# Down projection of a two-layer decoder trunk by seven block products over pairs of inner tiles

## The chip, the cores and the metric

The kernel runs on one core of one Trainium2 chip. Its time is the device time of one execution in microseconds (us); the median of three executions is given. TensorE does the matmuls (PE in the profile), with its weight loads beside them (PEld). VectorE is DVE, ScalarE is ACT, GpSimd is POOL, and SyncE (SP) issues most of the transfers.

## What is computed

The trunk has two layers over 1024 positions and 1024 channels. Each layer is a mixer followed by a gated MLP with a causal width-3 convolution. The change touches the MLP, above all its last product:

```python
def conv_ffn(x, norm_g, w_up, conv_w, conv_b, w_down):
    h = causal_depthwise_conv(rms_norm(x, norm_g) @ w_up, conv_w, conv_b)
    g, u = jnp.split(h, 2, axis=-1)
    return (jax.nn.silu(g) * u) @ w_down          # D_FF = 2816: 22 inner tiles of 128
...
for layer in range(2):
    x = x + mixer(layer, x)
    x = x + conv_ffn(x, ...)
```

## The kernel before

Activations lie transposed, channels on the partitions and positions along the row. All large products are float32 in two parts: a value is cut into a high part (rounded to the PE's fp32r) and a low part (the rest), and a product is three matmuls, high by high, high by low, low by high. A matmul is 128x128 weights by 512 positions.

**Weights.** SP loads 128x1024 tiles into a ring of three (`w_raw`), each after the tile three before it has been used up (L2029, L2056). ACT makes the high part (`w_hi`), POOL the low part (`w_lo`), both into rings of three tiles, which the MLP uses as six half tiles.

**Up projection** (`pe_ffn`, 22 steps j in each layer). A step makes gate rows and value rows of one inner tile. It is a 2x2 block product done with seven block products in place of eight: a11, s2, s3, s1, a22, a12, s4, in this order (`PRODS`). Each is 12 matmuls (`pe_product`, L1695). Their weights are quarters of two weight tiles (g and u) or sums s1 to s4 of quarters, which POOL makes (L1639 to L1664). ACT cuts the high parts (`act_cut`, L1631), POOL the low ones (`pool_low`, L1637). A half tile is cut when the product six before it is done, so the cuts run up to six products ahead.

**Behind the products** DVE adds the seven results into rows: ACT copies a11 to `ffn_v` (`act_p1`, L1845); DVE makes the U sums `dve_u2` and `dve_u3` (L1776, L1781), then the gate rows (`c22`, `c21`, `hg`: L1789, L1794, L1800) and the value rows (`c11`, `c12`, `hu`: L1809, L1813, L1820). Then comes the convolution: the centre tap on ACT (`act_center`, L1854) and two more taps on DVE (`dve_taps`, L1826 and L1828) for the gate side (m = 0) and the value side (m = 1); SiLU on ACT (L1860); the gating on DVE (`dve_gated`, L1835). Each engine's order is written out in `dve_ffn` and `act_ffn`. Two waits of PE matter below: product a22 of step j needs `dve_u3` of step j, and s1 of step j+1 needs `c12` of step j:

```python
            elif name == "a22":
                pe.wait_ge(parts, l * ALL_PARTS + part(j, "u3"))
```

ACT's order around it is, for step j: a cut, SiLU of j-1, `act_p1` of j (which waits for `c12` of j-1), the cut of s4 of j, the centre tap of the value side of j-1, the cut of a11 of j+1.

**Gated rows.** There are two buffers `ffn_gated` on the chip, so SP writes 20 of the 22 gated tiles to DRAM (`sp_gated_out`, L2061), between its two weight loads of a step, and they are read back for the down projection (`gated_in`).

**Down projection** (`pe_down`, L1748). The 22 inner tiles are taken in chunks of 4, 4, 4, 4, 2, 4. For each chunk and each of 8 output tiles PE adds up the chunk in PSUM, in one of four rooms in turn, and DVE adds the room to the residual `res` (`dve_down`, L1911, 48 per layer in the whole). Each inner tile is cut into high (ACT, L1876) and low (DVE, L1839); weights by ACT (L1891) and POOL (L1896). Layer 1 begins as output tiles of layer 0's last chunk are final: ACT and DVE normalise them, POOL adds squares (L438) and cuts the first weight tile of the mixer (L2039, L2041).

Of the kernel before, what the change touches and what calls it, by code (L numbers as in the profile page):

```python
# [14 lines left out]
P = 128  # L15
# [14 lines left out]
DOWN_ORDER = (FC - 2, 0, 1, 2, FC - 1, *range(3, FC - 2))  # L30
DOWN_SIZES = (4, 4, 4, 4, 2, 4)
LAST = len(DOWN_SIZES) - 1
ML_DV = 256
# [43 lines left out]
def program(nc, x_in, pos_in, wall, pool_w, params, lam4, consts, scratch, gated_rows, out):  # L77
    with ExitStack() as ctx:
# [188 lines left out]
        def td(n):  # L267

            return n - sum(min(max(n - t, 0), 2 * FC) for t in (T_FFN0, T_FFN1))
# [1120 lines left out]
        def act_pair_base(act, f, p):  # L1390

            if p:
                act.wait_ge(tt_made, f.l * 3 * KC // 2 + 3 * p - 1)
            evacuated(act, jobs[f"out{f.l}", 2 * p])
            act.activation(rbc[:, :], res[:, 2 * p, :], ACT.Copy, scale=gain(f, 2 * p)).then_inc(t_base, 1)

        def act_pair_high(act, f, p):

            act.wait_ge(tt_made, f.l * 3 * KC // 2 + 3 * p + 3)
# [53 lines left out]
        def dve_pair_sums(dve, f, p):  # L1453
# [52 lines left out]
        SLOTS = 8  # L1506
        STAGED = [p for p in range(FC) if DOWN_ORDER[p] < FC - 2]
# [17 lines left out]
        ALL_PARTS = len(FIRST_PARTS) + len(PARTS) * (FC - 1)  # L1525

# [3 lines left out]
        class Ffn:  # L1530


            def __init__(self, l):
# [20 lines left out]
                self.a = [at(f"ffn_gated{l}_{i}", [P, S], F32, r) for i, r in enumerate((r_m1, r_m2))]  # L1554
                self.hi = at(f"act_hi_buf{l}", [P, SLOTS, S], F32R, far)
                self.lo = at(f"act_lo_buf{l}", [P, SLOTS, S], F32R, far + 8 * K4)
                self.stage = at(f"act_stage{l}", [P, 2 * STAGES, S], F32, near)
                self.A = pj[:, self.late, 0:HALF]
# [12 lines left out]
            def g_tile(self, j):  # L1571

                return self.T0 + 2 * j + (j == 0)

            def u_tile(self, j):

                return self.T0 + 2 * j + (j != 0)

            def cut(self, t, w):

                q = (2 * (self.T0 % W_RING) + t) % (2 * W_RING)
# [28 lines left out]
            def gated_source(self, p):  # L1610

                if p in STAGED:
                    return self.stage[:, 2 * (STAGED.index(p) % STAGES), :]
                return self.a[DOWN_ORDER[p] % 2][:, :]
# [4 lines left out]
        def act_cut(act, f, t):  # L1619

            j, i = divmod(t, N_PROD)
            name = (PRODS if j else FIRST_PRODS)[i]
            if t < 2 * W_RING:
                act.wait_ge(tile_done, td(f.T0 - W_RING + t // 2 + 1))
            else:
                act.wait_ge(prod_done, f.l * N_PROD * FC + t - 2 * W_RING + 1)
            if name[0] == "a":
                raw_landed(act, f.g_tile(j) if name == "a22" else f.u_tile(j))
            else:
                act.wait_ge(s_made, f.l * 4 * FC + 4 * j + int(name[1]))  # L1630
# [16 lines left out]
        def pool_s2(pool, f, j):  # L1647
            raw_landed(pool, f.u_tile(j))
            pool.wait_ge(s_made, f.l * 4 * FC + 4 * j + 1)
            if j:  # L1650
                pool.wait_ge(c_ready, f.l * N_PROD * FC + prod(j - 1, "s2"))
            pool.tensor_tensor(wsum[1][:, :], wsum[0][:, :], f.source(j, "a11"), ALU.subtract).then_inc(s_made, 1)  # L1652

        def pool_s3(pool, f, j):
            raw_landed(pool, f.g_tile(j))
            raw_landed(pool, f.u_tile(j))
            if j:
                pool.wait_ge(c_ready, f.l * N_PROD * FC + prod(j - 1, "s3"))
            pool.tensor_tensor(wsum[2][:, :], f.source(j, "a11"), f.source(j, "a21"), ALU.subtract).then_inc(s_made, 1)  # L1659

        def pool_s4(pool, f, j):
            pool.wait_ge(s_made, f.l * 4 * FC + 4 * j + 3)
            pool.wait_ge(c_ready, f.l * N_PROD * FC + prod(j, "s1"))
            pool.tensor_tensor(wsum[0][:, :], f.source(j, "a12"), wsum[1][:, :], ALU.subtract).then_inc(s_made, 1)  # L1664

        def pe_room(pe, f, j, name):

            l = f.l
            if name == "a12":
                pe.wait_ge(p1_copied, l * FC + j + 1)  # L1670
            elif j and name == "s4":
                pe.wait_ge(parts, l * ALL_PARTS + part(j, "c22"))
# [1437 lines left out]
```

## Time and profile before

| | us |
|---|---|
| median of 3 executions (2168.45 to 2169.01) | 2168.55 |
| the profiled execution's own time | 2168.64 |
| its span in the trace | 2166.8 |
| PE busy | 2148.5 |
| DVE busy | 1326.5 |
| POOL busy | 1073.1 |
| ACT busy | 838.9 |

The span is that of the instructions; the time has 1.8 us around it. Matmuls are pipelined: the duration of one (389 ns) overlaps the next, so the rate is read from start to start. The granted TensorE clock is 0.997 of full speed over the whole span.

### The profile page before, as it was taken

What the parts mean: (1) busy time and instruction counts of PE and PEld (TensorE: products, weight loads), DVE (VectorE), ACT (ScalarE), POOL (GpSimd) and SP (SyncE); (2) the same over time, 40 slices, a digit from 0 to 9 for tenths busy, and PEclk for the clock granted to TensorE, in tenths of its full rate; (3) what the DMA queues carried; (4) which work ended last, traced back from release to release, by engine and by line L of the source; (5) the groups of instructions that cost most, each with busy time, mean ns of one, the idle gap of its engine ahead of it and who ended that gap; (6) DMA issues with size and microseconds to landing.
All of it is one profiled execution on the core that took longest, in us unless ns stands there. A gap on an engine that the chain in (4) does not pass through costs nothing. (4 is left out here: it accounts for less than half of the span.)

```text
span 2166.8 us, 26682 instructions
## 1 busy us (share of the span) xinstructions
PE 2148.5 (99%) x10219; PEld 1773.2 (82%) x10219; DVE 1326.5 (61%) x1425; ACT 838.9 (39%) x1312; POOL 1073.1 (50%) x664
## 2 busy tenths in 40 slices
PE   9999999999999999999999999999999999999999
PEld 8777778878888888888888898887788888888887
DVE  7766777567777777444544244286777777774442
ACT  6555452444443443111344433434444444441110
POOL 2222117677777773222543333267777777742220
PEclk9999999999999999999999999999999999999999
DMA  6111104022222224222321021030222222242221
GB/s 205 59 50 33 42 10 143 23 87 88 78 80 80 84 88 155 98 89 73 111 84 59 20 79 59 20 137 29 78 86 80 78 88 88 69 156 97 97 68 78
DMA packets 50429, 174.80 MB, mean 81 GB/s; under 512 B 6080, under 2 KB 8192, under 8 KB 50304
## 3 DMA queue, kind: packets, MB, share of 16 engines
q1 hardware_dynamic: 42816, 147.49, 20.5%
q10 hardware_dynamic: 7488, 25.61, 3.2%
q8 instruction: 82, 1.34, 0.3%
q14 instruction: 43, 0.35, 0.1%
HBM read 139.23 MB, written 29.66 MB: 78 GB/s over the span
## 5 line engine op out<-in xcount | busy, mean ns | idle before, releaser
L2039 POOL TENSOR_TENSOR w_hi<-w_raw,ones 128x1024 fp32r<-128x1024 f32 x54 | 106.1, 1965 | 494.1 <-PE pj L328 170.5
L1637 POOL TENSOR_TENSOR w_lo<-w_sum,w_hi 128x512 fp32r<-128x512 f32 x176 | 270.2, 1545 | 106.4 <-ACT w_hi L1631 106.4
L1896 POOL TENSOR_TENSOR w_lo<-w_raw,w_hi 128x1024 fp32r<-128x1024 f32 x44 | 106.0, 2409 | 342.0 <-ACT w_hi L1891 342.0
L1631 ACT ACTIVATE w_hi<-w_sum 128x512 fp32r<-128x512 f32 x176 | 106.6, 628 | 299.5 <-POOL w_sum L1652 170.3
L1706 PE MATMUL pj<-t_hi,w_hi 128*128 128x512 f32 x520 | 205.4, 395 | 7.6 <-DVE ffn_v L1781 7.6
L1706 PE MATMUL pj<-t_lo,w_hi 128*128 128x512 f32 x520 | 204.7, 394 | 0.0
L1706 PE MATMUL pj<-t_hi,w_lo 128*128 128x512 f32 x520 | 204.3, 393 | 0.0
L1637 POOL TENSOR_TENSOR w_lo<-w_raw,w_hi 128x512 fp32r<-128x512 f32 x132 | 172.7, 1309 | 63.4 <-ACT w_hi L1631 63.4
L1891 ACT ACTIVATE w_hi<-w_raw 128x1024 fp32r<-128x1024 f32 x44 | 46.6, 1059 | 318.7 <-PE dn L1748 168.7
L1706 PE MATMUL pj<-xa_hi,w_hi 128*128 128x512 f32 x348 | 135.8, 390 | 1.5 <-DVE xa_lo L1450 0.9
L1706 PE MATMUL pj<-xb_hi,w_hi 128*128 128x512 f32 x348 | 135.6, 390 | 1.6 <-DVE xb_lo L1450 0.9
L2041 POOL TENSOR_TENSOR w_lo<-w_raw,w_hi 128x1024 fp32r<-128x1024 f32 x54 | 135.0, 2501 | 4.2
L1706 PE MATMUL pj<-xa_hi,w_lo 128*128 128x512 f32 x348 | 135.4, 389 | 0.0
L1706 PE MATMUL pj<-xb_hi,w_lo 128*128 128x512 f32 x348 | 135.4, 389 | 0.0
L1706 PE MATMUL pj<-xa_lo,w_hi 128*128 128x512 f32 x348 | 135.4, 389 | 0.0
L1706 PE MATMUL pj<-xb_lo,w_hi 128*128 128x512 f32 x348 | 135.4, 389 | 0.0
L1839 DVE TENSOR_TENSOR act_lo_buf<-act_stage,act_hi_buf 128x1024 fp32r<-128x1024 f32 x40 | 80.2, 2009 | 80.0 <-ACT act_hi_buf L1876 80.0
L355 PE MATMUL pj<-xb_hi,w_hi 128*128 128x512 f32 x384 | 128.2, 415 | 0.0
L1631 ACT ACTIVATE w_hi<-w_raw 128x512 fp32r<-128x512 f32 x132 | 83.2, 631 | 113.6 <-PE pj L1706 113.6
L1706 PEld LDWEIGHTS pj<-t_hi,w_hi 128*128 128x128 f32 x520 | 98.7, 190 | 33.6 <-issue 9.1
L355 PE MATMUL pj<-xb_lo,w_hi 128*128 128x512 f32 x384 | 119.2, 392 | 0.0
L355 PE MATMUL pj<-xb_hi,w_lo 128*128 128x512 f32 x384 | 118.4, 390 | 0.0
(390 smaller groups left out, 5519.2 us busy)
## 6 DMA issues: line engine op xcount, KB each, us to landing
w_raw<-weights SPq DMA_DIRECT2D x187, 512.0 KB, 3.5
gated_rows<-ffn_gated SPq DMA_DIRECT2D x40, 512.0 KB, 2.6
act_stage<-gated_rows ACTq DMA_DIRECT2D x32, 512.0 KB, 4.5
x_first<-x_t SPq DMA_DIRECT2D x8, 512.0 KB, 7.7
res<-x_t SPq DMA_DIRECT2D x8, 512.0 KB, 6.6
act_stage<-gated_rows SPq DMA_DIRECT2D x8, 512.0 KB, 5.5
scratch<-res ACTq DMA_DIRECT2D x8, 512.0 KB, 2.6
res<-scratch SPq DMA_DIRECT2D x8, 512.0 KB, 7.0
```

The source lines that it names most:

```text
L355: ins = pe.matmul(o[:, t * HALF:(t + 1) * HALF], w, x[:, k, t * HALF:(t + 1) * HALF], start=(first and m == 0), stop=(last and m == 2))
L1631: act.activation(f.cut(t, whi), f.source(j, name), ACT.Copy).then_inc(c_high, 1)
L1637: pool.tensor_tensor(f.cut(t, wlo), f.source(j, name), f.cut(t, whi).bitcast(F32), ALU.subtract).then_inc(c_ready, 1)
L1706: ins = pe.matmul(o, f.cut(t, w)[:, k * P:(k + 1) * P], f.moving(name, x, k), start=(not more and k == 0 and q == 0), stop=(k == KC // 2 - ...
L1839: dve.tensor_tensor(f.lo[:, p % SLOTS, :], f.gated_source(p), f.hi[:, p % SLOTS, :].bitcast(F32), ALU.subtract).then_inc(act_lo, 1)
L1891: act.activation(whi[:, n % W_RING, :], raw[:, n % RAW_RING, :], ACT.Copy).then_inc(w_high, 1)
L1896: pool.tensor_tensor(wlo[:, n % W_RING, :], raw[:, n % RAW_RING, :], whi[:, n % W_RING, :].bitcast(F32), ALU.subtract).then_inc(w_ready, 1)
L2039: pool.tensor_tensor(whi[:, w, :], raw[:, r, :], ones[:, 0:1].to_broadcast([P, D]), ALU.mult).then_inc(w_high, 1)
L2041: pool.tensor_tensor(wlo[:, w, :], raw[:, r, :], whi[:, w, :].bitcast(F32), ALU.subtract).then_inc(w_ready, 1)
```

## The change

Inner tiles 4 to 19 (16 of 22) leave the plain chunks and are taken as 8 pairs. The plain chunks that stay are one of 4 inner tiles (20, 0, 1, 2) at the start and one of 2 (3 and 21) at the end. Two pairs and half of the output rows make a block: 8 blocks m per layer, each seven block products of 12 matmuls in the order `PRODS` (`pe_block`). Their weights are cut and summed by the same functions as the up projection's, whose steps j now run from 0 to 29.

- **Pair sums (T sums).** The moving side also needs sums. In the even steps j = 6 to 20 DVE makes four 128x512 sums in place in the two gated buffers (`dve_pair_t`), between the gate side's taps and `c12`. SP writes the two buffers out again (`sp_pair_out`, two transfers), between the step's two weight loads, the first after three sums, the second after four.
- **U sums first.** `dve_u2` and `dve_u3` of step j stand ahead of the gating of j-1. SP's write of a gated tile stands ahead of both weight loads of a step, no longer between them.
- **In the blocks** DVE adds each product into `u` or `res` (`dve_block`, seven additions of 1024 a block; in the first two blocks ACT copies the first); in the last two blocks three more, `res` plus `u`. ACT reads the pairs back from DRAM (`act_pair_load`) and cuts 1536 and 2048 positions of a pair per block (`act_pair_split`); DVE makes their low parts (`dve_pair_low_half`) between the additions.

```diff
-DOWN_ORDER = (FC - 2, 0, 1, 2, FC - 1, *range(3, FC - 2))
-DOWN_SIZES = (4, 4, 4, 4, 2, 4)
+DOWN_ORDER = (FC - 2, 0, 1, 2, 3, FC - 1)
+DOWN_SIZES = (4, 2)
+PAIR0 = 4
+N_PAIR = 8
+N_BLOCK = N_PAIR
...
+        def pe_block(pe, f, m, name):
...
+            if name == "a12":
+                if m < 2:
+                    pe.wait_ge(p1_copied, l * (FC + 2) + FC + m + 1)
+                else:
+                    pe.wait_ge(parts, l * LAYER_PARTS + block_part(m, "u1"))
+            elif name == "a22":
+                pe.wait_ge(parts, l * LAYER_PARTS + block_part(m, "e22"))
+            elif name == "s4":
+                pe.wait_ge(parts, l * LAYER_PARTS + block_part(m, "c22"))
...
+            else:
+                pe.wait_ge(parts, l * LAYER_PARTS + block_part(m - 1, {"a11": "a11", "s2": "u2", "s3": "e21", "s1": "c12"}[name]))
...
+        def dve_pair_t(dve, f, r):
+
+            b11, b12, b21, b22 = (f.ab[:, i, h * HALF:(h + 1) * HALF] for i in range(2) for h in range(2))
...
+            dve.tensor_tensor(b22, b22, b12, ALU.subtract).then_inc(tt_made, 1)
+            dve.wait_ge(tt_made, at0 + 1)
+            dve.tensor_tensor(b12, b12, b11, ALU.subtract).then_inc(tt_made, 1)
+            dve.wait_ge(tt_made, at0 + 2)
+            dve.tensor_tensor(b11, b11, b22, ALU.add).then_inc(tt_made, 1)
+            dve.wait_ge(tt_made, at0 + 3)
+            dve.tensor_tensor(b21, b21, b11, ALU.subtract).then_inc(tt_made, 1)
...
+        def dve_block(dve, f, m):
+
+            u = f.u[m % 2][:, :, :]
+            if m >= 2:
...
+                dve_block_add(dve, f, m, "u1", u, f.block_room("a11"))
...
+            dve_block_add(dve, f, m, "u2", u, f.block_room("s2"))
+            if m >= N_BLOCK - 2:
+                dve_block_done(dve, f, m, "u2")
+                for row, half in ((1, 1), (1, 0), (0, 1)):
+                    to = f.res_of(m, row, half)
+                    dve.tensor_tensor(to, u, to, ALU.add).then_inc(parts, 1)
...
+            dve_block_add(dve, f, m, "e22", f.res_of(m, 1, 1), f.block_room("s3"))
...
+            dve_block_add(dve, f, m, "c22", f.res_of(m, 1, 1), f.block_room("s1"))
+            if m + 2 < N_PAIR:
+                dve_pair_low_half(dve, f, m + 2, 0)
...
+            dve_block_add(dve, f, m, "e21", f.res_of(m, 1, 0), f.block_room("a22"))
...
+            dve_block_add(dve, f, m, "a11", f.res_of(m, 0, 0), f.block_room("a12"))
+            if m + 2 < N_PAIR:
+                dve_pair_low_half(dve, f, m + 2, 1)
...
+            dve_block_add(dve, f, m, "c12", f.res_of(m, 0, 1), f.block_room("s4"))
...
                 if j > 1:
                     dve_u2(dve, f, j)
                     dve_u3(dve, f, j)
+                    dve_gated(dve, f, j - 1)
...
                 dve_taps(dve, f, j, 0)
+                if j >= PAIR0 + 2 and j % 2 == 0:
+                    dve_pair_t(dve, f, (j - PAIR0 - 2) // 2)
                 dve_c12(dve, f, j)
                 dve_hu(dve, f, j)
                 dve_taps(dve, f, j, 1)
-                dve_gated(dve, f, j)
...
             for j in range(FC):
-                sp_up_load(sp, f, f.T0 + 2 * j)
                 if j >= 3:
                     sp_gated_out(sp, f, j - 3)
-                sp_up_load(sp, f, f.T0 + 2 * j + 1)
+                sp_load(sp, f.T0 + 2 * j)
+                if j - 3 > PAIR0 and j % 2 == 0:
+                    sp_pair_out(sp, f, (j - 3 - PAIR0) // 2)
+                sp_load(sp, f.T0 + 2 * j + 1)
...
         def pool_cut(pool, n, s, per):
-            if n >= W_RING:
+            if n == T_MIX1:
+                pool.wait_ge(prod_done, N_PROD * N_UP)
+            elif n >= W_RING:
                 pool.wait_ge(tile_done, td(n - W_RING + 1))
```

DVE at the end of an even step and the start of the next, before (layer 0; the names stand in the section on the kernel before):

```order
L1828 SCALAR_TENSOR_TENSOR dn<-ffn_hg_129,params,dn 128x1023
L1813 TENSOR_TENSOR ffn_hu_132<-pj,ffn_v_0_130 128x512
L1820 TENSOR_TENSOR ffn_hu_132<-ffn_hu_132,rms_bc 128x512
L1826 SCALAR_TENSOR_TENSOR dn<-ffn_hu_132,params,dn 128x1022
L1828 SCALAR_TENSOR_TENSOR dn<-ffn_hu_132,params,dn 128x1023
L1835 TENSOR_TENSOR ffn_gated_0_134<-ffn_silu_133,dn 128x1024
L1776 TENSOR_TENSOR ffn_v_0_130<-pj,ffn_v_0_130 128x512
L1781 TENSOR_TENSOR ffn_v_1_131<-pj,ffn_v_0_130 128x512
```

and the same place of DVE in the change (L1935 to L1941 are the T sums, L1868 and L1873 the U sums):

```order
L1920 SCALAR_TENSOR_TENSOR dn<-ffn_hg_129,params,dn 128x1023
L1935 TENSOR_TENSOR ffn_gated_134<-ffn_gated_134 128x512
L1937 TENSOR_TENSOR ffn_gated_134<-ffn_gated_134 128x512
L1939 TENSOR_TENSOR ffn_gated_134<-ffn_gated_134 128x512
L1941 TENSOR_TENSOR ffn_gated_134<-ffn_gated_134 128x512
L1905 TENSOR_TENSOR ffn_hu_132<-pj,ffn_v_0_130 128x512
L1912 TENSOR_TENSOR ffn_hu_132<-ffn_hu_132,rms_bc 128x512
L1918 SCALAR_TENSOR_TENSOR dn<-ffn_hu_132,params,dn 128x1022
L1920 SCALAR_TENSOR_TENSOR dn<-ffn_hu_132,params,dn 128x1023
L1868 TENSOR_TENSOR ffn_v_0_130<-pj,ffn_v_0_130 128x512
L1873 TENSOR_TENSOR ffn_v_1_131<-pj,ffn_v_0_130 128x512
L1928 TENSOR_TENSOR ffn_gated_134<-ffn_silu_133,dn 128x1024
```

Four instructions were added ahead of `c12`, and the gating moved from ahead of the U sums to behind them.

ACT in one block of the change (L1689 cuts weights, L2082 cuts a pair, L2061 to L2064 read pairs back):

```order
L1689 ACTIVATE w_hi<-w_sum_118 128x512
L2061 DMA pair_stage_0_142<-gated_rows 128x2048
L1689 ACTIVATE w_hi<-w_raw 128x512
L2082 ACTIVATE pair_0_148<-pair_stage_0_142 128x1536
L1689 ACTIVATE w_hi<-w_sum_119 128x512
L1689 ACTIVATE w_hi<-w_sum_120 128x512
L2082 ACTIVATE pair_0_148<-pair_stage_0_142 128x2048
L1689 ACTIVATE w_hi<-w_sum_118 128x512
L2063 DMA pair_stage_0_142<-gated_rows 128x512
L2064 DMA pair_stage_0_142<-gated_rows 128x1024
```

The rows are the cuts of s4, a11, s2, s3 and s1; the pair's larger cut stands between those of s3 and s1, where the up projection has nothing.

## Rows read from the trace of the kernel before

**Rows 1.** The page, part 1: busy us of PE, share of the span, instructions
```profile
PE 2148.5 (99%) x10219; PEld 1773.2 (82%) x10219; DVE 1326.5 (61%) x1425; ACT 838.9 (39%) x1312; POOL 1073.1 (50%) x664
```
**Rows 2.** PE's waits: us in total, times, longest
```profile
PE pj L1706 <- DVE ffn_v L1781: 7.6, 4, 3.6
```
**Rows 3.** The chain that ended last, layer 1: start, us, what
```profile
1550.85 373.38 PE pj L1706 x1632
...
1935.14 10.88 PE dn L1748 x48
```
**Rows 4.** Timeline of PE, layer 1: start, duration, engine, line, what
```profile
1714.33 0.39 PE L1706 MATMUL pj<-xa_hi,w_hi 128*128 128x512 f32 x1
...
1725.22 0.39 PE L1706 MATMUL pj<-t_hi,w_hi 128*128 128x512 f32 x1
...
1733.40 0.39 PE L1706 MATMUL pj<-xa_hi,w_hi 128*128 128x512 f32 x1
```
**Rows 5.** Timeline of DVE in the same step
```profile
1714.90 1.29 DVE L1828 SCALAR_TENSOR_TENSOR dn<-ffn_hg,params,dn 128x1023 f32<-128x1023 f32 x1
1716.10 0.69 DVE L1813 TENSOR_TENSOR ffn_hu<-pj,ffn_v 128x512 f32<-128x512 f32 x1
1716.82 1.53 DVE L1820 TENSOR_TENSOR ffn_hu<-ffn_hu,rms_bc 128x512 f32<-128x512 f32 x1
...
1722.35 1.22 DVE L1835 TENSOR_TENSOR ffn_gated<-ffn_silu,dn 128x1024 f32<-128x1024 f32 x1
...
1724.28 0.69 DVE L1781 TENSOR_TENSOR ffn_v<-pj,ffn_v 128x512 f32<-128x512 f32 x1
```
**Rows 6.** Timeline of POOL in the same step
```profile
1715.24 1.30 POOL L1637 TENSOR_TENSOR w_lo<-w_raw,w_hi 128x512 fp32r<-128x512 f32 x1 [0.73 <-ACT w_hi L1631]
1716.50 1.30 POOL L1664 TENSOR_TENSOR w_sum<-w_raw,w_sum 128x512 f32<-128x512 f32 x1
```
**Rows 7.** Timeline of ACT in the same step
```profile
1717.25 0.60 ACT L1845 ACTIVATE ffn_v<-pj 128x512 f32<-128x512 f32 x1
1717.89 0.63 ACT L1631 ACTIVATE w_hi<-w_sum 128x512 fp32r<-128x512 f32 x1
1718.42 1.19 ACT L1854 ACTIVATE dn<-ffn_hu,params 128x1024 f32<-128x1024 f32 x1
```
**Rows 8.** PE in step 1 of layer 0, where it waited for a U sum
```profile
439.51 0.47 PE L1706 MATMUL pj<-t_hi,w_hi 128*128 128x512 f32 x1 [0.24 <-DVE ffn_v L1781]
```
**Rows 9.** Timeline of SP in the same step: issue of two weight loads
```profile
1714.54 3.66 SPq L2056 DMA_DIRECT2D w_raw<-weights  x2
```
**Rows 10.** The page, part 6: transfers, KB each, median us from issue to landing
```profile
w_raw<-weights SPq DMA_DIRECT2D x187, 512.0 KB, 3.5
gated_rows<-ffn_gated SPq DMA_DIRECT2D x40, 512.0 KB, 2.6
```
**Rows 11.** Timeline of POOL, steps 1 and 2 of layer 0: low part of s4
```profile
438.37 1.28 POOL L1637 TENSOR_TENSOR w_lo<-w_sum,w_hi 128x512 fp32r<-128x512 f32 x1 [0.81 <-ACT w_hi L1631]
...
455.83 1.30 POOL L1637 TENSOR_TENSOR w_lo<-w_sum,w_hi 128x512 fp32r<-128x512 f32 x1 [0.80 <-ACT w_hi L1631]
```
**Rows 12.** Groups of DVE by line and form: count, busy us, mean ns, idle before
```profile
L1911 DVE TENSOR_TENSOR res<-pj,res 128x1024 f32<-128x1024 f32 x48 | 57.9, 1219 | 92.9 <-PE pj L1748 92.9
...
L968 DVE TENSOR_TENSOR o_normed<-o_tok,o_rstd 128x1024 f32<-128x1024 f32 x4 | 4.9, 1225 | 0.1
```
**Rows 13.** Groups of ACT by line and form: the cut of a weight tile
```profile
L1891 ACT ACTIVATE w_hi<-w_raw 128x1024 fp32r<-128x1024 f32 x44 | 46.6, 1059 | 318.7 <-PE dn L1748 168.7 <-PE pj L1748 143.8 <-PE pj L1706 6.1
```
**Rows 14.** Timeline of POOL into layer 1: square sum, then the first weight cut
```profile
1062.08 2.61 POOL L438 TENSOR_TENSOR ssum<-ssum,sq_tmp 128x1024 f32<-128x1024 f32 x1 [2.83 <-ACT sq_tmp L426]
1064.66 1.89 POOL L2039 TENSOR_TENSOR w_hi<-w_raw,ones 128x1024 fp32r<-128x1024 f32 x1
1066.62 2.39 POOL L2041 TENSOR_TENSOR w_lo<-w_raw,w_hi 128x1024 fp32r<-128x1024 f32 x1
```
**Rows 15.** Timeline of PE: its first matmul of layer 1
```profile
1074.76 0.28 PE L2310 MATMUL pj<-w_hi,xb_hi 128*128 128x264 f32 x1
```

More of the change, by code:

```diff
@@ L1525, in program, with block_parts, block_part, act_at @@
         ALL_PARTS = len(FIRST_PARTS) + len(PARTS) * (FC - 1)
+        def block_parts(m):
+            shared = ("v22", "v21", "v12") if m >= N_BLOCK - 2 else ()
+            return ("u1",) * (m >= 2) + ("u2",) + shared + ("e22", "c22", "e21", "a11", "c12")
+        def block_part(m, name):
+            return ALL_PARTS + sum(len(block_parts(i)) for i in range(m)) + block_parts(m).index(name) + 1
+        LAYER_PARTS = block_part(N_BLOCK - 1, "c12")
+        def act_at(p):
+            return p if p < DOWN_SIZES[0] else p + 2 * N_PAIR
+        def pair_at(q, part):
+            return DOWN_SIZES[0] + 2 * q + part
+        def out_at(j):
+            return j + 1 + 2 * max(0, (j - PAIR0) // 2)
         def chunk_at(c):
@@ L1737, in pe_down @@
                     pe.wait_ge(gated, f.l * FC + FC)
+                elif c == LAST and d < 4:
+                    pe.wait_ge(parts, f.l * LAYER_PARTS + block_part(N_BLOCK - 1, ("a11", "u2", "e21", "c12")[d]))
                 else:
@@ L1791, in dve_c21 @@
         def dve_c21(dve, f, j):
[L1792 removed]
+            dve.wait_ge(prod_done, f.l * N_PROD * N_UP + prod(j, "a22"))
             if j:
@@ L3011, in ffn, with plain @@
         tiles = [up[FC], up[0]] + [up[FC * m + j] for j in range(1, FC) for m in range(2)]
-        at = 0
-        for size in DOWN_SIZES:
-            part = np.stack([down[i] for i in DOWN_ORDER[at:at + size]])
-            part = part.reshape(size, P, size, KC // size, P).transpose(2, 1, 3, 0, 4).reshape(size, P, D)
-            tiles += list(part)
-            at += size
+        def plain(order):
+            size = len(order)
+            part = np.stack([down[i] for i in order])
+            return list(part.reshape(size, P, size, KC // size, P).transpose(2, 1, 3, 0, 4).reshape(size, P, D))
+        tiles += plain(DOWN_ORDER[:DOWN_SIZES[0]])
+        blocks = down[PAIR0:PAIR0 + 2 * N_PAIR].reshape(N_PAIR // 2, 2, 2, P, 2, 2, 2, P)
+        for c in range(N_PAIR // 2):
+            for k in range(2):
+                for row in (1, 0):
+                    tiles.append(blocks[c][:, :, :, k, :, row].transpose(2, 1, 3, 0, 4).reshape(P, D))
+        tiles += plain(DOWN_ORDER[DOWN_SIZES[0]:])
         return tiles
```

382 lines of the change are left out of this document (268 added, 114 removed).

## The prediction

> **What bounds the kernel now.** I read the page first. PE is busy for 2148.5 of 2166.8 us with 10219 matmuls [rows 1], and the chain of waits is PE alone through the MLP of layer 1, up projection and down projection alike [rows 3]. So time goes only where PE gets fewer or cheaper matmuls, and every wait put on PE costs its full length. The rate is the same in both stages: 48 matmuls in 10.88 us are 0.2267 us each [rows 3], and one step of the up projection, 84 matmuls from 1714.33 to 1733.40, is 19.07 us or 0.2270 each [rows 4]; a product of 12 is 2.72 us.
>
> The view to read next is PE's waits. The one large entry is on `dve_u3`, 7.6 us in four waits [rows 2]; in step 1 PE started product a22 0.15 us after that sum's end [rows 8]. In the steady step the sum (L1781) ends at 1724.97 and a22 starts at 1725.22 [rows 4, 5]: PE does not wait, but only 0.25 us are left. The change works just ahead of this sum.
>
> **Removed from PE.** Per layer 16 inner tiles x 8 outputs x 6 = 768 matmuls become 8 blocks x 84 = 672. That is 192 fewer in the kernel, at 0.2267 us: **-43.5 us**. The rate has no reason to differ: each product is again 12 matmuls of 512, each with its own weight load, as in the up projection.
>
> **T sums (16 times).** I follow one step with the clock of the steady step, in which a22 starts at 1725.22. The last gate tap ends at 1716.19 [rows 5]. A T sum reads both inputs from SBUF, as `hu` (L1820) does. That row shows what it costs beside POOL: 1.53 us, ending 0.55 after POOL's operation of 1716.50 to 1717.80 [rows 5, 6]; an addition with one input in PSUM takes 0.69 [rows 5]. So DVE and POOL take turns. The first T sum waits for POOL's operation that ends at 1716.54 [rows 6] and ends at 1717.09; POOL's own sum then runs to 1718.35; the second T sum ends at 1718.9. After that POOL has nothing: its next operation needs ACT's cut [rows 11], which stands behind `act_p1`, which waits for `c12`, which is behind the T sums. The last two take 0.69 and 0.1 between them, to 1720.5. Then in order: `c12` 0.69 to 1721.1, ACT's copy 0.60 and cut 0.63 to 1722.4, centre tap 1.19 to 1723.55 [rows 7] (`hu` is done by then), two taps of 1.29 to 1726.2, two U sums to 1727.6 [rows 5], PE at 1727.75. Against 1725.22 that is 2.5 us. It counts the U sums ahead of the gating: with the 1.22 us of L1835 [rows 5] ahead of them it would be 3.7. So 16 x 2.5 = **+40 us**. Bounds: if no T sum meets POOL they take 3.1 in place of 4.3, and `hu` is hidden, 1.3 us a time, 21 in all; if all four meet a POOL operation, 7.2, that is 5.4 a time, 86 in all.
>
> The Trainium skill, page "SBUF — State Buffer", section "Who interferes with whom", says that a DVE instruction with two SBUF inputs and a GpSimd instruction reading SBUF hold the shared pair for the whole instruction, whoever was first. By that rule the turns cannot be shortened, and the upper bound is a rival below.
>
> **The load behind them (14 times).** SP issues the T sums' two writes between the two weight loads. The second load, issued at the step's start in the trace (1714.54) [rows 9], now comes after the fourth T sum, at about 1721.2, behind two writes (2.6 each alone) and 3.5 to land [rows 10]. I put landing at 1725.5 to 1726. ACT cuts it into a11 some 6 us late, and stands there, with its later centre tap of the gate side behind four more cuts that need POOL. By the same counting that tap is 2.1 us late; the next step's U sums, now ahead of the gating, have 1.3 us to spare. 0.8 us remain: **+11 us** (0 to 28, for 2 us each). The loads that now stand behind a gated write are 7 us later and are not needed for over 12: nothing.
>
> **The blocks (16).** POOL, per block: 11 operations of 1.26 [rows 6] and three waits for ACT's cut of a fresh sum, 0.8 each [rows 11]. From one low part of s4 to the next it did this in 17.46 us when not held by PE, with one DVE operation in between [rows 11]; PE needs 19.04. A block adds pair low parts of 1536 and 2048 positions: at the 1.225 of an undisturbed 1024 [rows 12] about 1.7 and 2.2 us in which POOL is shut out, where the up projection had 1.1 that showed; and ACT's cut of 2048, 1.9 us by the 1.06 for 1024 [rows 13], between its cuts of s3 and s1. Together a cycle comes to about 20.2, 1.1 more than PE's. The six half tiles of lead hold that for some five blocks (a12 is ready 11.4 us ahead); in the sixth PE waits 1.4. In the seventh DVE is about 4.5 us behind when it reaches the three extra additions, which have two SBUF inputs and take turns with POOL, 7 us in place of 3.7; a22 waits for `e22` behind them, 8 us by my count, and 3 more follow up to the block's end and in the eighth. That is 12 per layer, **+24 us**. Bounds: the three additions undisturbed still make `e22` 1 us late in each of two blocks, 4 in all; with reading back a pair (1.75 MB) delaying weight loads as well, 25 per layer, 50.
>
> **Into layer 1.** Output tiles of the last chunk become final every 2.72 us, no longer 5.44. POOL cuts layer 1's first weight tile after the square sum of the fourth tile: square 2.61, then 1.96 and 2.39, in the trace 5.8 us before PE's first matmul [rows 14, 15]. DVE needs 1.22 [rows 12] and about 1.5 per tile, as much as PE. I get POOL ready 4 us after PE: **+4 us** (0 to 6). The tail after the last matmul stays.
>
> Hidden: the first block's pairs are cut during the plain chunk of 43.5 us, where DVE had a third free; stores fit between tiles at 2.6 us each.
>
> **Sum.** -43.5 + 40 + 11 + 24 + 4 = +35.5. Against the profiled execution's own 2168.64 (the median is 2168.55, the same) that is **2204 us**.
>
> **Rivals.**
>
> *The other side: the T sums nearly hidden.* If POOL's phase leaves them alone (3.1 us, 21 in all), the late load is absorbed, and the blocks cost their least, the sum is -43.5 + 21 + 0 + 4 + 2 = -16.5: 2152; with the first two smaller still (0.75 a time is the least, if the taps start earlier) 2143. For it: 1.3 us of slack comes with the new order, and DVE is busy only 61% [rows 1]. Against it: `hu` meets POOL in every steady step. The deciding point is the wait per T sum: with the blocks and layer 1 as forecast and no late load, 1.0 us; with these at their least, 2.3. Chance 0.22.
>
> *T sums as forecast, the rest at its least.* -43.5 + 40 + 4 + 2 = +2.5: 2171. It needs a POOL cycle under 19. Chance 0.14.
>
> *All four T sums take turns*, by the lock whatever POOL's phase: -43.5 + 86 + 11 + 30 + 4 = +88: 2256. Against it: POOL runs dry behind `c12`. It is the case that the rule of the Trainium skill (page "SBUF — State Buffer", above) would give if POOL always had work. Chance 0.09.
>
> *The change does less than it says*: the order shows 1344 block matmuls for the 1536 taken out, so this could only be a rate above 0.2267. At 0.230 it would add 4 us. Too small for a case of its own.
>
> **How the numbers follow.** The forecast has 0.55, its own range 2180 to 2235. The whole range 2148 to 2240 leaves out most of the turns rival and the lowest part of the first. A difference of 0.2% (4.3 us) is about what can be told from none. Faster by more: 0.22, from the first rival and little of the second. Within: 0.08, from the second. Slower: 0.70.
>
> **What would show it.** PE's waits on `dve_u3` (now L1873), about 16 of 2.5 us in odd steps 7 to 21; with rows of 0.1 us or none, the T sum step is wrong. Smaller waits on it in even steps 8 to 20: the late load. T sums of about 0.8, 1.8, 0.7, 0.7 us. PE waits in the blocks from the sixth on, above all on `e22` of the seventh; none there, and the POOL cycle is wrong. A gap before layer 1's first matmul that POOL's L2041 ends. What would make the whole wrong is PE idle of under 40 us.

## The result and the profile after

The changed kernel takes 2207.47 us (median of four executions, 2205.56 to 2209.51), the kernel before on the same chip 2168.77. The ratio is 1.0181, with a 95% interval of 1.0167 to 1.0195. The forecast was 2204 us.

The page's busy times, which answer to [rows 1]:

```profile
PE 2128.8 (96%) x10027; PEld 1747.9 (79%) x10027; DVE 1428.8 (65%) x1545; ACT 890.0 (40%) x1396; POOL 1257.0 (57%) x808
```

PE has the 192 matmuls fewer, but is busy only 96% of the span. Its waits, which answer to [rows 2] (us in all, times, longest):

```profile
PE pj L1764 <- DVE ffn_v L1873: 46.6, 30, 2.3
PE dn L1839 <- DVE res L1954: 8.4, 4, 4.0
PE pj L1839 <- DVE pair L1950: 7.7, 4, 3.1
PE pj L2565 <- issue: 4.2, 1, 4.2
PE pj L1839 <- issue: 1.6, 1, 1.6
```

The first was 7.6 us in four waits. From PE's first matmul of a stage to the first of the next (for the last stage to the end of the span), the time went here:

| stage (us) | before | after |
|---|---|---|
| up projection, layer 0 / layer 1 | 431.0 / 431.2 | 459.1 / 457.3 |
| down projection, layer 0 / layer 1 | 239.4 / 242.7 | 233.7 / 233.0 |
| of it the eight blocks | none | 164.1 / 164.4 |
| mixer of layer 1 | 418.1 | 420.4 |

At their rate of 0.2267 us the 672 matmuls of the blocks would take 152.3 us. One step with T sums (j = 16) on DVE, in order of time (start, duration, line, operation, tiles, and in brackets the idle time ahead and what ended it):

```profile
758.54 0.99 DVE L1935 TENSOR_TENSOR ffn_gated<-ffn_gated 128x512 f32<-128x512 f32 x1
759.57 1.67 DVE L1937 TENSOR_TENSOR ffn_gated<-ffn_gated 128x512 f32<-128x512 f32 x1
761.27 0.69 DVE L1939 TENSOR_TENSOR ffn_gated<-ffn_gated 128x512 f32<-128x512 f32 x1
762.00 0.69 DVE L1941 TENSOR_TENSOR ffn_gated<-ffn_gated 128x512 f32<-128x512 f32 x1
762.61 0.68 DVE L1905 TENSOR_TENSOR ffn_hu<-pj,ffn_v 128x512 f32<-128x512 f32 x1
763.33 0.69 DVE L1912 TENSOR_TENSOR ffn_hu<-ffn_hu,rms_bc 128x512 f32<-128x512 f32 x1
765.64 1.29 DVE L1918 SCALAR_TENSOR_TENSOR dn<-ffn_hu,params,dn 128x1022 f32<-128x1022 f32 x1 [1.62 <-ACT dn L2022]
...
768.95 0.69 DVE L1873 TENSOR_TENSOR ffn_v<-pj,ffn_v 128x512 f32<-128x512 f32 x1
```

On PE, ACT and POOL of the same step:

```profile
769.78 0.47 PE L1764 MATMUL pj<-t_hi,w_hi 128*128 128x512 f32 x1 [1.96 <-DVE ffn_v L1873]
...
763.38 0.60 ACT L2013 ACTIVATE ffn_v<-pj 128x512 f32<-128x512 f32 x1 [3.69 <-DVE ffn_hu L1905]
764.40 1.20 ACT L2022 ACTIVATE dn<-ffn_hu,params 128x1024 f32<-128x1024 f32 x1
768.12 0.63 ACT L1689 ACTIVATE w_hi<-w_raw 128x512 fp32r<-128x512 f32 x1 [2.51 <-DMA w_raw<-weights]
...
758.94 1.75 POOL L1722 TENSOR_TENSOR w_sum<-w_raw,w_sum 128x512 f32<-128x512 f32 x1
764.58 1.29 POOL L1695 TENSOR_TENSOR w_lo<-w_sum,w_hi 128x512 fp32r<-128x512 f32 x1 [3.89 <-ACT w_hi L1689]
```

The T sums take 1.0, 1.7, 0.7 and 0.7 us (forecast about 0.8, 1.8, 0.7, 0.7), POOL then has nothing for 3.9 us, and PE stands 1.96 us on `dve_u3`; so it does sixteen times in the odd steps 7 to 21 (once 2.31). ACT's row at 768.12 is the late weight tile, for which ACT stood 2.5 us. It returns as a second kind of wait in the even steps, ten of 0.2 to 1.2 us.

In the seventh block (m = 6) of layer 0, DVE:

```profile
1026.61 2.29 DVE L1950 TENSOR_TENSOR pair<-pair_stage,pair 128x2048 fp32r<-128x2048 f32 x1 [5.57 <-ACT pair L2082]
...
1032.59 6.75 DVE L1983 TENSOR_TENSOR res<-down_u,res 128x1024 f32<-128x1024 f32 x3
1039.37 2.55 DVE L1954 TENSOR_TENSOR res<-dn,res 128x1024 f32<-128x1024 f32 x2
```

PE waited 3.06 us for the first of these rows and 4.01 for `e22` behind the three additions.

Into layer 1 POOL's cut of the first weight tile ends, and PE starts 0.1 us later:

```profile
1093.69 3.21 POOL L2298 TENSOR_TENSOR w_lo<-w_raw,w_hi 128x1024 fp32r<-128x1024 f32 x1
1097.00 0.56 PE L2565 MATMUL pj<-w_hi,xb_hi 128*128 128x264 f32 x1 [4.17 <-issue]
```

### The profile page after: what moved, and what is told of

It is laid out like the page before. It is cut to its first block and busy times, and to the rows that moved or that the text cites. A ratio compares the mean times of both kernels' runs of the same rounds, so it can differ in the third digit from the quotient of the medians.

```text
span 2207.7 us, 26911 instructions
## 1 busy us (share of the span) xinstructions
PE 2128.8 (96%) x10027; PEld 1747.9 (79%) x10027; DVE 1428.8 (65%) x1545; ACT 890.0 (40%) x1396; POOL 1257.0 (57%) x808
## 5 line engine op out<-in xcount | busy, mean ns | idle before, releaser
L1695 POOL TENSOR_TENSOR w_lo<-w_sum,w_hi 128x512 fp32r<-128x512 f32 x240 | 362.0, 1517 | 211.0 <-ACT w_hi L1689 211.0
L1689 ACT ACTIVATE w_hi<-w_sum 128x512 fp32r<-128x512 f32 x240 | 146.3, 627 | 492.3 <-POOL w_sum L1710 223.3
L1695 POOL TENSOR_TENSOR w_lo<-w_raw,w_hi 128x512 fp32r<-128x512 f32 x180 | 236.5, 1321 | 107.4 <-ACT w_hi L1689 107.4
L1764 PE MATMUL pj<-t_hi,w_hi 128*128 128x512 f32 x520 | 210.5, 405 | 46.6 <-DVE ffn_v L1873 46.6
L1839 PE MATMUL dn<-pair,w_hi 128*128 128x512 f32 x512 | 159.1, 392 | 8.4 <-DVE res L1954 8.4
L1689 ACT ACTIVATE w_hi<-w_raw 128x512 fp32r<-128x512 f32 x180 | 111.4, 625 | 138.3 <-PE pj L1764 59.5
L2298 POOL TENSOR_TENSOR w_lo<-w_raw,w_hi 128x1024 fp32r<-128x1024 f32 x54 | 135.9, 2516 | 4.2
L1839 PE MATMUL pj<-pair,w_hi 128*128 128x512 f32 x384 | 120.1, 394 | 9.4 <-DVE pair L1950 7.7
L1839 PEld LDWEIGHTS dn<-pair,w_hi 128*128 128x128 f32 x512 | 96.8, 190 | 30.1 <-issue 10.0
```

Source lines behind the costliest of these rows:

```text
L1764: ins = pe.matmul(o, f.cut(t, w)[:, k * P:(k + 1) * P], f.moving(name, x, k), start=(not more and k == 0 and q == 0), stop=(k == KC // 2 - ...
L1839: ins = pe.matmul(room[:, d * HALF:(d + 1) * HALF], f.cut(t, w)[:, at0:at0 + P], f.pair_block(2 * c + q, x, name), start=(not more and q = ...
L2298: pool.tensor_tensor(wlo[:, w, :], raw[:, r, :], whi[:, w, :].bitcast(F32), ALU.subtract).then_inc(w_ready, 1)
```

## The experiments

The kernel before ran beside every experiment, so kernels are compared by their ratios to it; on these chips it took 2167 to 2170 us, and the changed kernel stands at about 2206. The blocks' column is their length in layer 0 / layer 1. A, B and C are the theories named in the expectation of each experiment, which was written before it ran.

| edit | median us | ratio, 95% | waits on `dve_u3`, us | blocks, us |
|---|---|---|---|---|
| the change | 2207.5 | 1.0181 (1.0167 to 1.0195) | 46.6 | 164.1 / 164.4 |
| T sums of one column | 2175.2 | 1.0042 (1.0025 to 1.0059) | 23.2 | 164.4 / 164.3 |
| loads first | 2197.1 | 1.0141 (1.0126 to 1.0156) | 36.7 | 164.3 / 164.4 |
| T sums moved | 2237.7 | 1.0325 (1.0309 to 1.0340) | 59.5 | 164.6 / 165.0 |
| T sums moved, loads first | 2156.2 | 0.9952 (0.9937 to 0.9967) | 6.6 | 164.9 / 163.8 |
| gating first | 2240.2 | 1.0359 (1.0298 to 1.0419) | 61.7 | 164.9 / 164.6 |
| additions spread | 2207.7 | 1.0189 (1.0174 to 1.0204) | 47.1 | 164.8 / 164.6 |
| same, low parts last | 2204.4 | 1.0166 (1.0147 to 1.0186) | 47.2 | 160.5 / 161.7 |
| pair's second cut behind s1 | 2197.9 | 1.0148 (1.0131 to 1.0164) | 44.7 | 159.1 / 158.8 |
| layer 1's cut first | 2203.4 | 1.0167 (1.0150 to 1.0184) | 45.5 | 164.4 / 163.9 |
| six edits | 2137.6 | 0.9869 (0.9850 to 0.9889) | 5.3 | 153.0 / 159.2 |
| four of them, second cut behind s2 | 2142.6 | 0.9875 (0.9853 to 0.9896) | 6.6 | 158.4 / 158.5 |
| six edits, second cut behind s2 | 2132.6 | 0.9845 (0.9830 to 0.9859) | 5.4 | 152.3 / 152.3 |

### The T sums without their work

```diff
-            b11, b12, b21, b22 = (f.ab[:, i, h * HALF:(h + 1) * HALF] for i in range(2) for h in range(2))
+            b11, b12, b21, b22 = (f.ab[:, i, h * HALF:h * HALF + 1] for i in range(2) for h in range(2))
```

> Edit: the four T sums are made on one column of each half tile, so this kernel leaves out the T sums' work and keeps their order, their waits and their two writes to HBM. Theory A (the T sums' time on DVE, through c12, ACT's centre tap and the U sums, is what PE waits for in the odd steps): the sixteen waits of 1.96 us on dve_u3 (L1873) in odd steps vanish, -31 to -34 us; the late load comes some 3.5 us earlier, so that most of its 11.6 us goes too (-8 to -12); about five of the half-clock spells per layer that follow such waits go with them (-6 to -13). Sum 2150 to 2162 us. Rival B (POOL's making of the low parts sets the pace of the up projection, the T sums only coincide with it): the waits stay on the same places at about their length, 2195 to 2207 us. Rival C (the waits of the odd steps come from the T sums, those of the even steps from the load's place behind the two writes whatever the sums take): 2165 to 2175 us, the even-step waits stay near 1.1 us each.

Measured 2175.2 us, C's case (0.2 above its range). The waits of the odd steps are gone but for one of 0.3 us, and the kernel is 30 us shorter by the ratios. Those of the even steps stayed, and there are now fourteen, of 1.2 to 1.95 us, 18 us in all where the change had 10: they do not need the time that the T sums take. That it is the load that sets them the next run shows. DVE's rows of one such step, and POOL's beside them:

```profile
707.02 0.46 DVE L1935 TENSOR_TENSOR ffn_gated<-ffn_gated 128x1 f32<-128x1 f32 x1
707.52 1.22 DVE L1937 TENSOR_TENSOR ffn_gated<-ffn_gated 128x1 f32<-128x1 f32 x1
708.77 0.16 DVE L1939 TENSOR_TENSOR ffn_gated<-ffn_gated 128x1 f32<-128x1 f32 x1
708.96 0.16 DVE L1941 TENSOR_TENSOR ffn_gated<-ffn_gated 128x1 f32<-128x1 f32 x1
...
707.42 1.29 POOL L1722 TENSOR_TENSOR w_sum<-w_raw,w_sum 128x512 f32<-128x512 f32 x1
```

One column takes 0.16 us alone and 1.22 us beside POOL, to within 0.03 us of POOL's end. So DVE and POOL take turns by whole instructions when both of DVE's inputs lie in SBUF. That is what the Trainium skill says (page "SBUF — State Buffer", section "Who interferes with whom"), and the trace agrees. In the change it bears on the first two of the four sums, since POOL then has nothing to do until `c12` is made.

### Both loads ahead of the writes

```diff
+                sp_load(sp, f.T0 + 2 * j + 1)
                 if j - 3 > PAIR0 and j % 2 == 0:
                     sp_pair_out(sp, f, (j - 3 - PAIR0) // 2)
-                sp_load(sp, f.T0 + 2 * j + 1)
```

> Edit: SP issues both weight loads of the step before the two writes of the T sums. Theory A (ACT's cut of the late weight tile is what delays the even steps' U sums): the even-step waits on dve_u3 (five per layer, 11.6 us in all) fall under 0.3 us each, the odd-step waits stay at 1.96 us; up to four half-clock spells go too (-0 to -6). 2190 to 2197 us. Rival B (the even-step waits are what the T sums leave DVE behind by, the load only coincides): they stay, 2205 to 2208 us. Rival C (the loads now share HBM and queues with other traffic at another place and something new is late): over 2208 us.

2197.1 us, the upper end of A. No wait of an even step is left; the odd ones stay at 1.96. PE runs at half clock for a short spell behind some of its waits (the last section has the rows); there were twelve such spells in the MLP in place of eleven, so none of these went with the waits.

### The T sums moved

```diff
                 dve_c11(dve, f, j)
+                dve_pair_t(dve, f, j, (0,))
                 dve_taps(dve, f, j, 0)
-                if j >= PAIR0 + 2 and j % 2 == 0:
-                    dve_pair_t(dve, f, (j - PAIR0 - 2) // 2)
                 dve_c12(dve, f, j)
                 dve_hu(dve, f, j)
+                dve_pair_t(dve, f, j, (1, 2, 3))
```

> Edit: of the four T sums the first stands behind c11, the other three between hu and the centre tap of the value side, no longer all between the gate taps and c12. Theory A (their 4.1 us delay c12, ACT's copy and cut, hu and the centre tap, and 1.6 us of DVE's idle before that tap lies unused behind them): c12 starts with the gate taps' end, three sums of 0.7 to 1.7 us run where DVE had been idle for 1.3 to 1.6 us, and the odd-step waits of 1.96 us fall to between 0 and 1.2; with them most of the even-step ones (the load still behind the writes): -20 to -40 us, 2167 to 2187 us. Rival B (it is the length of the DVE row per step, wherever the sums stand): the waits stay within 0.3 us, 2200 to 2210 us. Rival C (behind c11 the first sum meets POOL or waits for the pair's write to land, and gate taps are late instead): waits of 1.5 us or more remain in odd steps, 2195 to 2215 us.

2237.7 us, 31 more and outside all three. The waits of the odd steps are gone but for one of 0.4 us, as A had it; but there are fourteen of 3.7 to 3.9 us in the even steps. SP, ACT, POOL and DVE of one pair of steps:

```profile
730.22 1.05 SPq L2312 DMA_DIRECT2D gated_rows<-ffn_gated  x2
731.37 0.47 SPq L2287 DMA_DIRECT2D w_raw<-weights  x1
...
736.34 0.63 ACT L1689 ACTIVATE w_hi<-w_raw 128x512 fp32r<-128x512 f32 x1 [7.17 <-DMA w_raw<-weights]
...
737.04 1.29 POOL L1695 TENSOR_TENSOR w_lo<-w_raw,w_hi 128x512 fp32r<-128x512 f32 x1 [7.40 <-ACT w_hi L1689]
...
748.05 1.29 DVE L1918 SCALAR_TENSOR_TENSOR dn<-ffn_hg,params,dn 128x1022 f32<-128x1022 f32 x1 [6.65 <-ACT dn L2025]
```

The T sums end later, the writes wait for them, and the load waits behind the writes. ACT stands 7.2 us at a tile that lands 5 us after its issue, POOL behind ACT, and DVE stands 6.65 us until the next step's centre tap, which ACT makes behind cuts that need POOL. The sums no longer delayed PE themselves; the load behind their writes did.

> Edit: two of the edits tried so far at once, the T sums moved (one behind c11, three behind hu) and both weight loads ahead of their writes. Alone the first cost 30 us (waits of 3.9 us in the even steps, ACT 7.2 us at a weight tile that had not landed) and the second gave 9 us. Theory A (moved T sums are themselves hidden, it was only the load behind their writes that came 3 us later still): of the 46.6 us of waits on dve_u3 (L1873) under 7 remain, all in steps 1 and 2, and the blocks stay as they were: 2207 - 34 - 12 - 8 (half-clock spells) = about 2153, 2146 to 2160 us. Rival B (the 3.9 us also have to do with DVE's longer row behind hu): waits of 1 us or more stay in even or odd steps, 2165 to 2195 us.

With both edits 2156.2 us, A's case and below the kernel before: 6.6 us are left on `dve_u3`, 4.9 of them in steps 1 and 2. Alone one edit gave 9 us and the other cost 31; together they give 50. All but 1.6 us of the T sums' waits lay in their place and in SP's order; the blocks are as long as in the change.

### One part undone: the gating ahead of the U sums

```diff
                 if j > 1:
+                    dve_gated(dve, f, j - 1)
                     dve_u2(dve, f, j)
                     dve_u3(dve, f, j)
-                    dve_gated(dve, f, j - 1)
```

> Edit: undoes one part of the change alone, DVE again gates (1.22 us) before it makes the two U sums of the next step. Theory A (the U sums stand at the end of the chain, so all of the 1.2 us comes on top): waits of 3.1 to 3.2 us in the odd steps, 1.0 to 1.2 us more in the even ones, step 2 again 3.5: 16 x 1.2 + 12 x 1.1 + 2 x 1.3 = 35 us, and half-clock spells up to 10 more: 2238 to 2255 us. Rival B (the waits end with something else, POOL or the load, that stands still while DVE gates): under 2225 us.

The odd waits are 3.28 us, the 1.3 more that A had; but the even ones fell to 0.3 or less, against A. The likely reason is that the longer pair of steps gives ACT and POOL the time that the late load had taken; no run tests it. Two executions took 2227.5 and 2227.9 us, two 2252.6 and 2252.7, with mean clocks of 0.986 and 0.971, hence the wide interval; the median of 2240.2 is in A's range, but lies between the two pairs, near no execution. The profile is of one of the first. By their time against the change's this part is worth about 20 us, by that of the other two about 45.

### The blocks: the three extra additions

In the last two blocks each of the three extra additions stands behind one of the sums (`extra` makes one of them), in place of all three ahead of `e22`:

```diff
-            if m >= N_BLOCK - 2:
-                dve_block_done(dve, f, m, "u2")
-                for row, half in ((1, 1), (1, 0), (0, 1)):
...
+            extra(1, 1, "e22")
             dve_block_prod(dve, f, m, "s1")
...
+            extra(1, 0, "v22")
...
+            extra(0, 1, "v21")
```

> Edit: the three extra additions of the last two blocks stand one each behind e22, c22 and e21, no longer all ahead of e22. Theory A (they delay e22 by their 6.75 us in one row): the waits of 4.0 and 2.9 us on res (L1954) and of 0.8 us in the blocks m=6 and m=7 go, with the half-clock spell behind two of them (-3), but later sums of these blocks (a11, a12, the s products' evictions) are then later by 2 to 5 us and some of it may come back: 2196 to 2201 us. Rival B (POOL's cycle of about 20.2 us sets the end of the blocks, the additions only show it): PE's wait moves to a12 or s4 of the same blocks at the same total, 2205 to 2208 us.

2207.7 us: B's number, but not by POOL's cycle. The waits on `e22` went, and one of 5.6 us a layer came 10 us later, at the first product of the eighth block, because DVE now stood at the low part of a plain tile:

```profile
1046.99 1.44 DVE L2017 TENSOR_TENSOR act_last<-act_stage,act_last 128x1024 fp32r<-128x1024 f32 x1 [6.20 <-ACT act_last L2051]
...
1045.38 0.63 ACT L1690 ACTIVATE w_hi<-w_sum 128x512 fp32r<-128x512 f32 x1 [2.71 <-POOL w_sum L1718]
...
1050.81 1.19 PE L1840 MATMUL pj<-pair,w_hi 128*128 128x512 f32 x2 [5.62 <-issue]
```

With the additions as just shown, the low parts of the two plain tiles now move from the seventh block to the eighth:

```diff
-            elif m == N_BLOCK - 2:
+            elif m == N_BLOCK - 1:
                 dve_gated_low(dve, f, DOWN_SIZES[0])
...
-            elif m == N_BLOCK - 2:
+            elif m == N_BLOCK - 1:
                 dve_gated_low(dve, f, DOWN_SIZES[0] + 1)
```

> Edit: the extra additions one at a time as in the kernel before this one, and the low parts of the two plain tiles in the last block, no longer in the one before it. Theory A (in that kernel DVE stood 6.2 us at the first of these low parts, which waits for ACT's cut, which stands behind a cut that waits for POOL, and so the gain of spreading the additions was given back as the wait of 5.6 us): the 5.6 us are gone and only some of the 4.0 + 0.8 us come back elsewhere: -6 to -11 us over the two layers, 2195 to 2200 us. Rival B (POOL's cycle of 20.2 us has used up the lead by then, whatever DVE does): a wait of 3 to 5 us on POOL's or DVE's part stays in block m=6 or 7, 2204 to 2208 us.

2204.4 us, the lower end of B's range, and by its interval not told from the change. The 5.6 us are gone, as A had it, and the blocks themselves are about 3 us shorter a layer; but 1.9 us came back ahead of the last chunk, and 3.1 us on the pair's low part stayed in the seventh block, the wait of 3 to 5 us that B had.

### The blocks: ACT's cut of 2048 positions

```diff
-                    if i == 4 and q < N_PAIR:
+                    if i == 5 and q < N_PAIR:
                         act_pair_split(act, f, q, 1)
```

> Edit: ACT cuts the second half of a pair (2048 positions) behind the cut of s1, no longer between those of s3 and s1. Theory A (this cut lengthens POOL's cycle, POOL's cycle is what makes the block sums late): POOL's cycle falls by 0.8 to 1.5 us, the waits on res in m=6 and 7 fall by 2 to 4 us per layer; the second half's low part comes later, which it can since s2 is the last product to need it: 2198 to 2204 us. Rival B (the second half's low part is itself what product s2 waits for, the waits of 0.9 and 3.1 us on pair L1950 in blocks 4 and 6): these waits grow by 1 to 3 us in each of four or more blocks per layer, 2212 to 2225 us.

2197.9 us, A's case by POOL's cycle and within 0.1 us by the total, but the waits that A named, those on `res`, fell by only 1 us (8.4 to 7.4). It was the waits on the pair's low part that went, from 7.7 to 0.3 us, though the cut stands later in ACT's order. ACT's pair cut and POOL's low parts of s3 and s1 in the sixth block of the change:

```profile
1003.72 1.90 ACT L2082 ACTIVATE pair<-pair_stage 128x2048 fp32r<-128x2048 f32 x1
...
1003.89 1.30 POOL L1695 TENSOR_TENSOR w_lo<-w_sum,w_hi 128x512 fp32r<-128x512 f32 x1 [0.80 <-ACT w_hi L1689]
1006.21 2.88 POOL L1695 TENSOR_TENSOR w_lo<-w_sum,w_hi 128x512 fp32r<-128x512 f32 x1 [1.02 <-ACT w_hi L1689]
```

and with the cut moved:

```profile
1001.12 1.90 ACT L2082 ACTIVATE pair<-pair_stage 128x2048 fp32r<-128x2048 f32 x1
...
1000.77 2.55 POOL L1695 TENSOR_TENSOR w_lo<-w_sum,w_hi 128x512 fp32r<-128x512 f32 x2 [0.80 <-ACT w_hi L1689]
```

In the change ACT's cut of s1 stands behind the 1.90 us, and POOL is idle for 1.02 us until it is made. From one sum s4 to the next POOL takes 20.4 us in the change (mean of six, 910.27 to 1032.52) and 19.5 here over the same six (910.27 to 1027.34), 19.2 in the middle three. As POOL ran ahead again, ACT's cut of the pair and DVE's low part came earlier in time, and PE no longer waited for them: those waits came from POOL's cycle. The waits of 2.9 us on `e22` stayed.

### Into layer 1, and all of it

Layer 1's first cut stands ahead of the square sums of output tiles 1 to 3, which now come one weight tile later:

```diff
-                if n == T_MIX1:
-                    for c in range(1, 4):
-                        add_squares(pool, 2, c)
                 if n == T_MIX1 + 1:
-                    for c in (4, 5):
+                    for c in range(1, 6):
```

> Edit: POOL cuts layer 1's first weight tile before the square sums of output tiles 1 to 3. Theory A (the gap of 4.2 us before layer 1's first matmul is POOL's weight cut behind a square sum that waits for a late output tile): the gap falls to 0.5 us or less, and the mixer is as long as before or up to 2 us longer, as its first statistics come later: 2202 to 2206 us. Rival B (the gap is the last output tile's own path through DVE and ACT, the cut only ends at the same time): the gap stays over 3 us, 2206 to 2209 us.

2203.4 us, A's case. The 4.2 us are gone, and a wait of 2.35 us on the second weight tile, behind the square sums, came. Yet the mixer is only 0.5 us longer than in the change (420.9 for 420.4): there the same matmuls ran at half clock behind the 4.2 us and lost about as much. The total's interval overlaps that of the change.

> Edit: all of it together: both loads before the writes, the T sums moved, the pair's second cut behind that of s1, the extra additions one at a time, the plain tiles' low parts in the last block, layer 1's first cut before the square sums. Theory A (the causes are separate and add up): waits on dve_u3 under 8 us in all against 46.6, those of the blocks under 5 against 18, gap into layer 1 under 1: 2207 - 35 (T sums) - 10 (load) - 10 (pair cut) - 8 (additions) - 4 = about 2140, between 2132 and 2155 us; it would beat the kernel before the change. Rival B (with the T sums and additions out of the way the POOL-ACT-DVE cycle takes over and PE waits for low parts): 2160 us or more, with new waits that c_ready or POOL ends.

2137.6 us, A's case. In layer 1's blocks a wait of 2.9 us on the pair's low part is left. In the next two kernels the second cut stands behind that of s2 (`i == 3`), where ACT had 2.7 us of idle:

> Edit: of the edits of the fastest kernel so far only those that move something on ACT, SP and the T sums: T sums moved, loads ahead of the writes, the pair's second cut behind that of s2; in the blocks the three extra additions stand in one row ahead of e22 again, as in the change, and the plain tiles' low parts as there. Layer 1's first weight tile is cut ahead of all five square sums. Theory A (POOL's cycle, 20.4 us a block in the change and 19.3 in the fastest kernel, came down by the cut's place alone; the additions' own price is what they delay e22 by in the last two blocks): no waits on pair, one wait on e22 of 2 to 4 us in m=6 and 0.8 in m=7, 3 to 5 us a layer, 2138 to 2143 us less 1 to 3 for layer 1's cut: 2136 to 2141 us. Rival B (spreading the additions was needed for POOL's cycle too, with which they take turns): POOL's cycle over 19.6 us and waits on pair as well, 2144 to 2152 us. Rival C (DVE now has the lead to hide the row of additions): no wait over 1 us in the blocks, 2128 to 2133 us.

2142.6 us: A's waits (3.0 and 0.8, in layer 1 with 1.6 more), 1.6 us above its range. No wait on the pair is left; the first wait in the blocks, whose length is 6 us over 152.3, is that on `e22` behind the row of additions.

> Edit: as the kernel with all six edits, but a pair's second cut stands one place earlier than in the change (behind the cut of s2, where ACT had been idle for 2.7 us), one plain tile's low part in each of the last two blocks, and two square sums of layer 1 one weight tile later. Theory A (what is left in the blocks is the order on ACT: the 2048 cut fits into the idle of 2.7 us and makes the second half's low part earlier): the waits of 0.3 and 2.9 us on pair and of 1.9 + 0.6 us ahead of the last chunk go, the 2.4 us of w_lo too: 2137.6 - 5 to 8 = 2130 to 2133 us. Rival B (POOL's cycle is longer than PE's whatever ACT does): waits of 2 to 4 us per layer stay in the sixth to eighth block, 2135 to 2139 us. Rival C (the pair's load has not landed by then, 6.5 us for 1 MB): ACT and POOL behind it stand, over 2140 us.

2132.6 us, A's case, the fastest: 0.9845 of the kernel before. Its busy times and largest waits:

```profile
PE 2109.8 (99%) x10027; PEld 1739.2 (82%) x10027; DVE 1449.6 (68%) x1545; ACT 896.0 (42%) x1396; POOL 1281.9 (60%) x808
```

```profile
PE pj L1765 <- DVE ffn_v L1874: 5.4, 5, 2.2
PE dn L2578 <- DVE res L2126: 3.7, 1, 3.7
PE pj L1809 <- issue: 2.4, 2, 1.7
```

The eight blocks take 152.3 us in both layers, PE without a wait, the value of 672 matmuls at 0.2267. The six edits' 2.4 us on the second weight tile are gone, as A had it, but the 3.7 us took their place: PE waits for an output tile, and runs at half clock behind that wait. From its first matmul of layer 1 it needs 27.0 us for 156 matmuls, with the six edits 23.7, so that this part of the edit cost 3 us.

## Why the prediction was right

The forecast of 2204 missed by 3.5 us of 38.7. By its terms, from the spans, whose difference is 40.9 (a wait is counted from PE's start to start, less 0.2267, so that the one shown as 1.96 us costs 2.12):

| term | forecast | measured |
|---|---|---|
| matmuls removed | -43.5 | -43.5 |
| T sums, 16 | +40 | +34 (16 x 2.12) |
| late load | +11 | +11.6 (10 waits) |
| blocks | +24 | +23.7, of it 3.4 at half clock |
| into layer 1 | +4 | +4.2, and 2.3 at half clock in the mixer |
| step 2, with the U sums first | not in it | -2.6 |
| half clock in the up projection | not in it | +9.3 |

That leaves 1.9 us unassigned. Where PE waits and for what was forecast rightly, but for the waits on the pair's low part. That the total is so close is in part luck: without the half clock the waits come to 67.5 us where the forecast had 79, and the half clock, which it had not, added 15.

- **T sums.** Right in place, mechanism and each sum's time. The chain was counted 0.4 us too long: the four sums take 4.07 us to the start of `c12` and not 4.3, and ACT's copy, cut and tap follow at 0.5 us from start to start, where their full 0.60 and 0.63 had been added. The one-column run and the move both took the odd-step waits away.
- **Late load.** The sum is right, the count was fourteen of 0.8 and is ten of 1.2. That the sum came out is luck. The cause is shown: with the load ahead of the writes these waits are gone. That a T sum placed better makes it worse was not foreseen.
- **Blocks.** POOL's cycle of 20.2 is 20.4, and the three additions' 7 us are 6.75. The cycle's parts are not as counted: 17.46 + 1.7 + 2.2 - 1.1 gives the 20.2 with nothing for ACT's cut of 2048, but with that cut moved the cycle is 19.2 to 19.5, so the cut is about 1 us of it and the other parts are 0.7 to 1 us less than counted. And the step "a22 waits for `e22` behind them, 8 us by my count" did not hold: 4.0 and 2.9. PE had by then already stood 0.9 us in the fifth block and 3.1 in the seventh on the second half of a pair's low part, which product s2 needs, a dependency that was not followed. Those waits go with POOL's cycle, the one on `e22` goes when the additions are spread. In the sixth, where 1.4 were forecast, it did not wait. The total of the blocks came out by errors that cancel.
- **Into layer 1.** POOL's weight cut ended the gap, as said. The half clock behind the gap was not in the forecast; when the order was changed, a wait for the second weight tile took its place.
- **Clock.** Missed, 15 us in all. It hid that the T sums' term was 6 us too large and the blocks' waits nearly 4.
- **The rival on the other side** came near in time once the T sums were moved and the loads put first, 2156 us for its 2152, but not by its sum: it had 21 us for the T sums and 4 for the blocks, and in that kernel the T sums leave 1.6 us of waits and the blocks cost as much as in the change.

## What to carry to other kernels

When work is put into an engine's row, price it together with the queue behind it: here the sums were nearly free in DVE's idle time, but the transfers that wait for them held a weight load in the same queue, and the two edits, of which apart one cost 31 us and the other gave 9, gave 50 together. Where an in-order engine serves two chains (ACT for pairs and for weights), a long operation belongs into its idle stretch, not between two cuts that another engine waits for one after the other; the wait may show on a tile of another chain, here the pair's. A move that gives nothing has often only uncovered the next wait in that engine's row.

## What the runs showed of the hardware

After many waits of some 2 us PE's next matmuls run at half clock: in the change's up projections after 9 of the 18 waits of 1.9 to 2.4 us, and after none of the ten of 1.2 us or less in the even steps. The granted clock is 0.50 there, 1.2 of 2.4 GHz (windows of 3 us: busy time and number of operations of each engine, clock, DMA share, GB/s), and eight matmuls follow at 0.427 us from start to start:

```profile
560.00:563.00 3.00, 3.00 (x8) 2.32 (x9) 1.48 (x2) 0.11 (x1) 2.66 (x3) 0.50 0.45 164
771.00:774.00 3.00, 3.00 (x15) 2.47 (x14) 1.52 (x3) 0.63 (x1) 2.07 (x3) 1.00 0.78 249
```

Both follow a wait of 1.96 us, so the wait's length alone doesn't decide it. Most spells cost 1.6 to 1.7 us. The kernel before has two in the MLP, behind its waits of 3.5 us (about 5 us together), the change eleven (about 18), the kernel with the T sums moved alone eighteen (over 30), the fastest two (about 3). A wait shown as 1.96 us can so cost 3.7. The change has one more at the start of layer 1's mixer, behind the 4.2 us: there matmuls of 264 positions follow at 0.22 us, for 0.12 in the kernel before.

The gating-first kernel's executions differ by 25 us on one chip, with mean clocks of 0.986 and 0.971. More such spells would explain it, but the longer executions have no trace here, so that stays open. What else decides whether a spell follows a wait stays open too.
